# Fourteen column tiles of an input projection, in pairs by seven block products

## The reference

```
p   = x @ w_in                      # 1024 x 1024 times 1024 x 3072
y_A = RWKV-7 time mixing of p[:, :1408]      (token shift, delta rule)
y_B = Griffin RG-LRU of p[:, 1408:1920]      (conv of width 4, gates, scan)
y_C = stick-breaking attention of the rest   (q, k, v of 384 columns each)
x   = LayerNorm(alpha * x + concat(y_A, y_B, y_C) @ w_out)
x   = LayerNorm(alpha * x + grouped top-2 MoE(x))
```

## Time and profile before

| | us |
|---|---|
| median of three runs | 1342.16 |
| the profiled execution | 1342.95 |
| its span, first to last instruction | 1341.2 |
| PE busy | 1242.6 |
| DVE busy | 468.9 |
| ACT busy | 381.1 |
| POOL busy | 121.0 |
| matmuls of the column tiles (L205) | 293.9 |

### The profile page before, as it was taken

The page is one execution under the profiler, slowest core; times in us unless marked ns, Lnnn a source line. Parts: engine busy times, 40 slices in busy tenths (PEclk is TensorE's granted clock), DMA queues, the critical chain, the costliest instruction groups (busy, mean ns, idle before and its releaser), DMA issues.

```text
span 1341.2 us, 23288 instructions
## 1 busy us (share of the span) xinstructions
PE 1242.6 (93%) x9734; PEld 602.4 (45%) x9734; DVE 468.9 (35%) x833; ACT 381.1 (28%) x571; POOL 121.0 (9%) x206
## 2 busy tenths in 40 slices
PE   7999999999989999998999956999999999999980
PEld 3444444444557777775445532333333333333320
DVE  3035301244357777774364353111111111111117
ACT  1034402333145565555222122111111111111114
POOL 1000000000021221220000001010101010101010
PEclk9999999999989999999999977999999999999995
DMA  5110001010000001001704019776799499397226
GB/s 220 32 47 31 32 32 47 32 31 16 0 2 3 34 4 34 4 3 65 267 6 157 28 44 354 275 273 197 268 313 312 148 319 367 101 369 254 55 38 259
DMA packets 61013, 170.19 MB, mean 127 GB/s; under 512 B 3184, under 2 KB 3312, under 8 KB 60928
## 3 DMA queue, kind: packets, MB, share of 16 engines
q1 hardware_dynamic: 54384, 145.31, 29.0%
q0 software_dynamic: 6544, 23.63, 7.4%
HBM read 144.29 MB, written 24.64 MB: 126 GB/s over the span
## 4 chain that ended last, share of the span: by engine, by line
PE 84%; DVE 6%; DMA 4%; ACT 3%; issue 2%; POOL 0%; SPq 0%; POOLq 0%; DVEq 0%; ACTq 0%
PE PS L1829 31%; PE PS L205 19%; PE PS L1300 8%; PE PS L214 3%; PE PS L659 3%; PE PS L994 2%; PE PS L678 2%; PE PS L1003 2%; PE PS L1013 2%; PE PS L1822 2%; DMA YT<-x1d,RK 1%; PE PS L348 1%; PE PS L1440 1%; PE PS L734 1%; DMA XS<-in_xT 1%
## 5 line engine op out<-in xcount | busy, mean ns | idle before, releaser
L205 PE MATMUL PS<-XS 128*128 128x512 f32 x672 | 293.9, 597 | 7.6 <-DMA XS<-in_xT 7.1
L1829 PE MATMUL PS<-XS,YT 128*64 128x512 f32 x656 | 287.9, 596 | 3.5 <-DMA SQ<-in_w_upx 2.6
L1829 PE MATMUL PS<-SQ,YT 128*64 128x512 f32 x488 | 216.4, 597 | 0.0
L1829 PE MATMUL PS<-RK,YT 128*64 128x512 f32 x672 | 211.1, 593 | 0.0
L205 PEld LDWEIGHTS PS<-XS 128*128 128x128 f32 x672 | 127.1, 191 | 172.7 <-issue 163.9
L1829 PEld LDWEIGHTS PS<-XS,YT 128*64 128x64 f32 x656 | 88.9, 137 | 185.4 <-issue 180.8
L1300 PE MATMUL PS<-SQ,YT 128*128 128x512 f32 x256 | 114.0, 594 | 0.6 <-issue 0.6
L1917 DVE TENSOR_TENSOR YT<-YT,PS 128x256 f32<-128x256 f32 x42 | 15.8, 418 | 274.7 <-PE PS L1829 274.7
L1829 PEld LDWEIGHTS PS<-RK,YT 128*64 128x64 f32 x672 | 65.9, 137 | 74.7 <-issue 74.7
L1300 PEld LDWEIGHTS PS<-SQ,YT 128*128 128x128 f32 x256 | 47.7, 190 | 56.7 <-issue 56.5
L1829 PEld LDWEIGHTS PS<-SQ,YT 128*64 128x64 f32 x488 | 66.4, 138 | 0.0
(11 more groups left out here) (386 smaller groups left out, 1591.2 us busy)
## 6 DMA issues: line engine op xcount, KB each, us to landing
RK<-in_w_down SPq DMA_DIRECT2D x6, 2048.0 KB, 12.6
XS<-in_w_in SPq DMA_DIRECT2D x21, 512.0 KB, 3.3
XS<-in_w_gate SPq DMA_DIRECT2D x5, 2048.0 KB
XS<-in_w_upx SPq DMA_DIRECT2D x5, 2048.0 KB
XS<-in_w_down SPq DMA_DIRECT2D x5, 2048.0 KB
RK<-in_w_gate SPq DMA_DIRECT2D x5, 2048.0 KB, 19.7
SQ<-in_w_gate SPq DMA_DIRECT2D x4, 2048.0 KB
RK<-in_w_upx SPq DMA_DIRECT2D x4, 2048.0 KB, 19.7
```

Of the source, the lines that this page charges most:

```text
L205: m = e.matmul(acc[:, half * HB:(half + 1) * HB], XS[:, 8 + n % 4, kt * P:(kt + 1) * P], XS[:, kt, half * HB:(half + 1) * HB], start=kt == ...
L1829: ins = e.matmul(acc[r, :], rows[:, r], third_cols(n, k, at, HB), start=start, stop=stop)
```

## The change

Two column tiles a (= n) and b (= n + 1) are computed together for n = 0, 2, ..., 12, that is for the tiles 0 to 13. The 256 columns by 1024 tokens are seen as a 2 by 2 block product: the contraction is cut into channels 0 to 511 and 512 to 1023 (a1, a2 of tile a; b1, b2 of tile b), the tokens into two halves. Instead of eight block products it takes seven (the Winograd form of Strassen's scheme), each of four matmuls 128x128 by 128x512 into one PSUM quarter of 512 columns. The four quarters of PS0 and PS1 are used in turn, one for each product.

- `x_sums` on DVE, ahead of `masks_dve`: sixteen subtractions of 128x512 give four sums of quarters of x, kept in SQ[:, 0:8].
- `weight_sums` on POOL, seven times: four additions or subtractions of 128x512 for each pair.
- `pair_pe` makes the seven products; `pair_act` copies the first from PSUM; `pair_dve` adds the six others to the rows in SBUF with seven TENSOR_TENSOR of 128x512 (product 4 is added twice).
- The RWKV rows lie in YT or TT now, not in PSUM, when ACT and DVE make the token shift.
- The load of w_in tile 1 is issued between x tiles 3 and 4.
- The pieces of LRU and RWKV after tile n run inside the pair: on PE after the second product (n) and after the fourth (n + 1); on ACT both after the copy of the first product; on DVE ahead of the additions (n) and after the fifth of them (n + 1).
- Seven semaphores are renamed or reused; tiles 14 to 20 and the v columns are computed as before.

```diff
-                if ct == 0:
-                    for kt in range(KT):
+                if ct < 2:
+                    for kt in range(4 * ct, 4 * ct + 4):
                         e.dma_start(XS[:, kt, :], t["xT"][kt]).then_inc(s_x[kt], 16)
...
+        def x_sums(e):
+            for k in range(4):
+                wait(e, s_x[k], 16)
+                e.tensor_tensor(XSUM[0][:, k, :], XQ[0, 1][:, k, :], XQ[0, 0][:, k, :], ALU.subtract).then_inc(s_ts, 1)
+            for k in range(4):
+                wait(e, s_x[4 + k], 16)
+                wait(e, s_ts, 4 + k)
+                e.tensor_tensor(XSUM[1][:, k, :], XQ[1, 1][:, k, :], XSUM[0][:, k, :], ALU.subtract).then_inc(s_ts, 1)
+            for k in range(4):
+                e.tensor_tensor(XSUM[2][:, k, :], XQ[1, 1][:, k, :], XQ[0, 1][:, k, :], ALU.subtract).then_inc(s_ts, 1)
+            wait(e, s_ts, 8)
+            for k in range(4):
+                e.tensor_tensor(XSUM[3][:, k, :], XQ[1, 0][:, k, :], XSUM[1][:, k, :], ALU.subtract).then_inc(s_ts, 1)
+
+        def weight_sums(e, p):
+            n, a1, a2, b1, b2, s1, s2, s4 = weights_of(p)
+            for i in range(2):
+                wait(e, s_w[(n + i) % 4], 16 * ((n + i) // 4 + 1))
+            if p >= 2:
+                wait(e, s_pp, n - 2)
+            e.tensor_tensor(s1, b1, b2, ALU.add).then_inc(s_ss, 1)
+            wait(e, s_ss, 4 * p + 1)
+            e.tensor_tensor(s2, s1, a1, ALU.subtract).then_inc(s_ss, 1)
+            wait(e, s_ss, 4 * p + 2)
+            e.tensor_tensor(b1, a1, b1, ALU.subtract).then_inc(s_ss, 1)
+            e.tensor_tensor(s4, a2, s2, ALU.subtract).then_inc(s_ss, 1)
+
+        def pair_pe(e, p, after):
...
+            product(0, a1, XQ[0, 0]).then_inc(s_mp, 1)
...
+            product(1, a2, XQ[1, 0]).then_inc(s_mp, 1)
+            after(n)
+            wait(e, s_w[(n + 1) % 4], 16 * ((n + 1) // 4 + 1))
+            wait(e, s_ts, 8)
+            wait(e, s_ss, 4 * (p + 1))
+            wait(e, s_md, 7 * (p - 1) + 6)
+            product(2, s2, XSUM[1]).then_inc(s_mp, 1)
+            wait(e, s_ts, 12)
+            wait(e, s_md, 7 * p)
+            product(3, b1, XSUM[2]).then_inc(s_mp, 1)
+            after(n + 1)
+            wait(e, s_me, p + 1)
+            product(4, s1, XSUM[0]).then_inc(s_mp, 1)
+            wait(e, s_ts, 16)
+            wait(e, s_md, 7 * p + 2)
+            product(5, b2, XSUM[3]).then_inc(s_pp, 1)
+            wait(e, s_md, 7 * p + 1)
+            product(6, s4, XQ[1, 1]).then_inc(s_pp, 1)
+
+        def pair_act(e, p, after):
...
+            wait(e, s_mp, 5 * p + 1)
+            wait(e, s_pd, r)
+            e.copy(A[:, 0:HB], quarter(p, 0)).then_inc(s_me, 1)
+            after(n)
+            after(n + 1)
+            if r >= 0:
+                wait(e, s_derived, 1)
+                wait(e, s_md, 7 * (p + 1))
+                for i, x in enumerate((A, B)):
+                    e.activation(RW[:, r + i, :], x, ACT.Identity, scale=v1(V_NMU + r + i)).then_inc(s_pa, 1)
+
+        def pair_dve(e, p, after):
...
+            after(n)
+            wait(e, s_me, p + 1)
+            wait(e, s_mp, 5 * p + 3)
+            add(A[:, HB:S], 2, A[:, 0:HB])
+            wait(e, s_md, d0 + 1)
+            add(A[:, 0:HB], 1, A[:, 0:HB])
+            wait(e, s_mp, 5 * p + 4)
+            wait(e, s_pd, r)
+            add(B[:, 0:HB], 3, A[:, HB:S])
+            wait(e, s_mp, 5 * p + 5)
+            wait(e, s_md, d0 + 3)
+            add(B[:, HB:S], 4, B[:, 0:HB])
+            add(A[:, HB:S], 4, A[:, HB:S])
+            after(n + 1)
+            wait(e, s_pp, n + 1)
+            wait(e, s_md, d0 + 5)
+            add(B[:, 0:HB], 5, B[:, 0:HB])
+            wait(e, s_pp, n + 2)
+            add(A[:, HB:S], 6, A[:, HB:S])
+            if r >= 0:
+                for i, x in enumerate((A, B)):
+                    wait(e, s_pa, r + i + 1)
+                    e.scalar_tensor_tensor(RW[:, r + i, 1:S], x[:, 0:S - 1], v1(V_MU + r + i), RW[:, r + i, 1:S],
+                                           ALU.mult, ALU.add).then_inc(s_pd, 1)
...
         def _(e):
             masks_pool(e)
+            for p in range(PAIRS):
+                weight_sums(e, p)
             mats_pool(e)
...
         def _(e):
+            x_sums(e)
             masks_dve(e)
             lru = [lru_dve(e, u) for u in range(2)]
```

More of the change, by code:

```diff
@@ L115, in layer_kernel @@
         s_masksd = sem("masks_built_dve")
-        s_x = [sem(f"x_loaded{i}") for i in range(NT)]
+        s_x = [sem(f"x_or_sums_loaded{i}") for i in range(NT)]
         s_w = [sem(f"w_in_loaded{i}") for i in range(4)]
@@ L121, in layer_kernel @@
         s_pe = sem("proj_copied_by_act")
+        s_ts, s_ss = sem("x_sums_dve"), sem("weight_sums_pool")
+        s_mp, s_me, s_md = sem("quarter_products_in_psum"), sem("quarters_copied_act"), sem("quarters_added_dve")
         s_ld, s_la, s_lp = sem("lru_dve"), sem("lru_act"), sem("lru_pe")
@@ L149, in layer_kernel @@
         s_ya, s_yd, s_ys = sem("y_act"), sem("y_dve"), sem("y_stored")
-        s_gt = [sem(f"sums_loaded{i}") for i in range(NT)]
         s_tick = [sem("sp_passed_wait"), sem("pool_passed_wait")]
@@ L185, in proj_sp @@
                 e.dma_start(XS[:, 8 + k, :], t["w_v"][:, (k - 1) * S:k * S]).then_inc(s_w[k], 16)
-        def proj_free(e, n):
[L189 to L194, removed]
+        FIRST_PAIR, PAIRS = 0, 7
+        XSUM = [SQ[:, 2 * i:2 * i + 2, :].rearrange("p a b -> p (a b)").rearrange("p (k c) -> p k c", k=4) for i in range(4)]
@@ new lines, in layer_kernel, with weights_of, pair_rows @@
+        XQ = {(j, k): XS[:, 4 * j:4 * j + 4, k * HB:(k + 1) * HB] for j in range(2) for k in range(2)}
+        WSUM = YT[:, 0:3, :].rearrange("p a b -> p (a b)").rearrange("p (s i c) -> p s i c", s=2, i=3)
+        def weights_of(p):
+            n = FIRST_PAIR + 2 * p
+            a, b = [XS[:, 8 + (n + i) % 4, :] for i in range(2)]
+            s1, s2, s4 = [WSUM[:, p % 2, i, :] for i in range(3)]
+            return n, a[:, 0:HB], a[:, HB:S], b[:, 0:HB], b[:, HB:S], s1, s2, s4
+        def pair_rows(p):
+            n = FIRST_PAIR + 2 * p
+            return (YT[:, 3 + n, :], YT[:, 4 + n, :]) if n < LRU_T else (YT[:, 7, :], TT[:, 2, :])
@@ new lines, in quarter, with product @@
+        def quarter(p, i):
+            q = 7 * p + i + 1
+            return PS[q // 2 % 2][:, q % 2 * HB:(q % 2 + 1) * HB]
+        def pair_pe(e, p, after):
+            n, a1, a2, b1, b2, s1, s2, s4 = weights_of(p)
+            def product(i, left, right):
+                for k in range(4):
+                    m = e.matmul(quarter(p, i), left[:, k * P:(k + 1) * P], right[:, k, :], start=k == 0, stop=k == 3)
+                return m
+            wait(e, s_md, 7 * (p - 1) + 3)
+            wait(e, s_w[n % 4], 16 * (n // 4 + 1))
+            if p == 0:
+                for k in range(4):
+                    wait(e, s_x[k], 16)
+            product(0, a1, XQ[0, 0]).then_inc(s_mp, 1)
+            wait(e, s_md, 7 * (p - 1) + 5)
+            if p == 0:
+                for k in range(4, KT):
+                    wait(e, s_x[k], 16)
+            product(1, a2, XQ[1, 0]).then_inc(s_mp, 1)
[16 more added lines that the diff above has]
+            product(6, s4, XQ[1, 1]).then_inc(s_pp, 1)
@@ new lines, in pair_act @@
+        def pair_act(e, p, after):
+            n, r = FIRST_PAIR + 2 * p, FIRST_PAIR + 2 * p - LRU_T
+            A, B = pair_rows(p)
+            wait(e, s_mp, 5 * p + 1)
[8 more added lines that the diff above has]
+                    e.activation(RW[:, r + i, :], x, ACT.Identity, scale=v1(V_NMU + r + i)).then_inc(s_pa, 1)
@@ new lines, in pair_dve, with add @@
+        def pair_dve(e, p, after):
+            n, r = FIRST_PAIR + 2 * p, FIRST_PAIR + 2 * p - LRU_T
+            A, B = pair_rows(p)
+            d0 = 7 * p
+            def add(to, i, other):
+                e.tensor_tensor(to, quarter(p, i), other, ALU.add).then_inc(s_md, 1)
+            after(n)
[22 more added lines that the diff above has]
+                                           ALU.mult, ALU.add).then_inc(s_pd, 1)
@@ new lines, in pair_at, with paired @@
+        def pair_at(n):
+            p = (n - FIRST_PAIR) // 2
+            return p if (n - FIRST_PAIR) % 2 == 0 and 0 <= p < PAIRS else None
+        def paired(n):
+            return FIRST_PAIR <= n < FIRST_PAIR + 2 * PAIRS
+        def proj_free(e, n):
+            m = n - 2
+            if paired(m):
+                wait(e, s_md, 7 * PAIRS - 1)
+            elif LRU_T <= m < RW_END:
+                wait(e, s_pd, m - LRU_T + 1)
+            elif m >= RW_END:
+                wait(e, s_pe, m - RW_END + 1)
@@ L201, in proj_pe @@
                 for half in range(2):
+                    if half and paired(n - 2):
+                        wait(e, s_md, 7 * PAIRS)
                     for kt in range(KT):
@@ L261, in own @@
                 wait(e, s_ld, n[0])
-            wait(e, s_pe, LRU_T)
+            wait(e, s_md, 14)
             own()
@@ L989, in sba_pe @@
```

(39 more changed lines are left out.)

## The result

The changed kernel takes 1353.25 us (median of four runs, 1353.16 to 1355.20), the kernel before 1342.66 us (four runs, 1341.47 to 1344.11). The ratio is 1.0084, with a 95% interval of 1.0069 to 1.0099: slower by 10.6 us. The profiled execution took 1353.28 us, its span is 1351.5 us. The forecast was 1347.5 us in 1337 to 1354. The direction and the kind of mechanism held. The size did not: the kernel lost 10.6 us where 4.8 were forecast, outside the forecast's own 1345 to 1350, and the time is that of rival 2, in which VectorE and GpSimd wait for each other in full (1353).

The account below looks back on a forecast made before the run. PE's matmuls were taken to bound the kernel. Pairs 0 and 1 +11.7 - 3.4, pairs 2 to 4 +4.0, pairs 5 and 6 -6.9 gave +5.4 us, median 1347.5 us, range 1337 to 1354.

Parts of the forecast that it names:

- rival 2: DVE and POOL wait for each other in full: +11 us after pair 1, 1353 us in all; chance 0.14.
- The saved work: Projection on PE: a pair takes 24.0 us where two tiles took 27.5; seven pairs save 24.0 us.
- The start: Pair 0: PE stands 7.4 us before P5, behind DVE's sums of x and masks; +8.3 us after pair 1.
- POOL beside DVE: Pairs 0 and 1: POOL's weight sums delay DVE's sums of x by 2.5 us, bounds 0 and 5 us.
- with all: End of pair 0 at 53 us as upper bound, where 50.3 us was forecast.
- The clock: PE after each long wait: 1.7 us for half clock, bounds nothing and twice that.
- Rival 3: Clock stays at 2.4 GHz over the three waits and POOL finds gaps: -4.1 us, 1338 us; chance 0.11.
- Pairs 2 to 4: Pairs beside the LRU: save 10.3 us of matmuls, lose 14.3 us to waits of 3.7 and 8.4 us and clock.
- The sum: All terms up to tile 14: +11.7 - 3.4 + 4.0 - 6.9 = +5.4 us.
- Given back: After tile 14: the prediction had what follows unchanged and shifting with PE, so nothing given back.
- Rival 1: POOL does not delay DVE: +1.0 us in all, 1343.2 us, counted as no change; chance 0.22.
- Rival 4: DVE's queue does not hold PE, only saved matmuls count: 24.0 less 3.4 us, 1321.6 us; chance 0.05.

Follow-up runs that it names:

- e9: e8 with the mask building in two parts, between the additions of P4 and P5 of pair 0 and after its last addition: 1321.19 us.
- e6: Changed kernel with masks_dve between the additions of pair 0 and those of pair 1: 1344.5 us, ratio 1.0011 to the kernel before.
- e5: Changed kernel without GpSimd's weight sums, so the projection is wrong: 1366.6 us, not comparable; tile 14 starts at 218.05 us, not 227.87.
- e4: Changed kernel with fourteen more float32 matmuls into an unused PSUM quarter between P4 and P5 of pair 0: 1352.55 us.
- e1: Changed kernel with masks_dve ahead of x_sums on VectorE: 1349.08 us, ratio 1.0059 to the kernel before.
- e7: Changed kernel with masks after pair 0's additions, GpSimd's pair 1 sums held, and the LRU's second half one tile later: 1329.48 us.
- e8: e7 with the convolution of the LRU's second half one place later on VectorE, behind the additions of P4 of pair 3: 1324.53 us.
- e2: Changed kernel with GpSimd's weight sums of pair 1 held until the second addition of pair 0: 1350.39 us, ratio 1.0063 to the kernel before.
- e3: Changed kernel with the LRU's second half tied to tiles 8, 9, 10 and not 7, 8, 9: 1339.43 us, ratio 0.9979 to the kernel before.

## Why the prediction was right, and where its sizes were off

**The saved work** is as forecast: pair 1, without a wait, goes from 54.79 to 78.82 us, 24.0 us. e9 shows that all seven pairs can run without a hole behind the arrival of x.

**The start.** P1, which needs the last tile of x, starts at 18.28 us (18.1 forecast). The order of DVE's queue is the cause of the hole (e6), and without POOL the hole is 7.1 us (e5; 7.4 forecast). The term that was mis-sized is the lock, "POOL beside DVE": 2.5 us were taken, 5.5 measured. The row of a scan that lost 0.46 us was read as the price of a meeting. By the times in the rows it was more likely one caught halfway, since the scan began at 396.02 us and the POOL copies behind it only at 396.62; this was not tested. In the changed kernel eight subtractions lost about 4.3 us to POOL's four sums of pair 1, about one microsecond for each sum. Pair 0 ended at 54.79 us, 4.5 us after the 50.3 forecast: 3.0 us are the lock, 1.3 us the clock. It also ended after the 53 us that the prediction gave as its worst case, "with all". That sum holds the lock in full but the clock at 1.7 us only, although the clock's own bound was twice that.

The Trainium skill (SBUF — State Buffer, section Summary: rules for kernel authors) says of a DVE instruction with two SBUF inputs and a GpSimd instruction that reads SBUF that the second one to issue "fully blocks" until the first finishes. Measured, DVE lost 1.0 us to a POOL sum of 1.27, so this wording gave the better price. Rival 2, built on it, met the time in part by luck: it had 11 us after pair 1 and 7 over pairs 2 to 4, and 12.7 and 6.0 were measured.

**The clock.** Forecast 1.7 us for each long wait, 5.1 in all; by the distances in PE's timeline it was 3.0, 1.4 and 2.5 us, 6.9 in all. e4 takes 2.9 us off at the first hole. Rival 3, that the clock stays, is out for these three waits. The 1.7 us came from the spacing of the first records at the kernel's start, where the profile's granted clock reads 1.00, so that row had not shown a price of the half clock.

**Pairs 2 to 4.** Pair 3 took 35.2 us (106.63 to 141.81), forecast 35.1; pair 4 took 37.8, forecast 36.1. The holes of 4.2 and 9.2 us were forecast as 3.7 and 8.4. From the end of pair 1 to that of pair 4 it is 100.8 us, forecast 98.8, before 94.8. Of these 2.0 us, 1.2 are the longer holes and 0.5 the clock. Behind the holes stands the lock again: the second token shift took 2.29 us instead of 1.28 in both pairs, and e5, without POOL, has holes of 3.2 and 7.3 us.

**The sum** at tile 14: 5.4 forecast, 4.5 more at the start and 2.0 more in pairs 2 to 4 give 11.9 us, where 12.1 were measured. The 0.2 us are about what starts in the timeline and in the chain differ by.

**Given back.** The prediction let what follows tile 14 shift with PE. With 12.1 us and nothing given back the time would have been about 1354.7 us, outside the range of 1337 to 1354; that the measured time is inside it is owed to this stretch, which nobody forecast. From tile 14 to the delta rule the two kernels run alike. In its first block they do not. The first and second block's POOL work, before and after the change:

```profile
373.00 1.62 POOL L617 TENSOR_TENSOR XS<-RK,pc 128x384 f32<-128x384 f32 x2 [367.69 <-PE PS L214]
395.05 1.62 POOL L617 TENSOR_TENSOR XS<-RK,pc 128x384 f32<-128x384 f32 x2 [17.66 <-PE PS L734]
```
```profile
385.05 1.62 POOL L762 TENSOR_TENSOR XS<-RK,pc 128x384 f32<-128x384 f32 x2 [195.73 <-PE PS L359]
405.87 1.63 POOL L762 TENSOR_TENSOR XS<-RK,pc 128x384 f32<-128x384 f32 x2 [16.42 <-PE PS L879]
```

The block takes 22.05 us before and 20.82 after. PE stands in it for about 3.2 us in both. Before, the clock read 0.50 when it went on the earlier trace rows; in the changed kernel it read 1.00 for the first two microseconds (same columns as above):

```profile
390.00:392.00 2.00, 1.69 (x44) 1.00 0.00 0
392.00:394.00 2.00, 1.40 (x41) 0.53 0.04 8
```

It fell some two microseconds of work later. That this is why the block is shorter is read from the rows and not tested. Nothing in the change aims at it; e1 to e7 have 22.4 to 22.6 us for the block, e9 22.05 and e8 21.0. It is part of why times and tile 14 differ by 1 to 2 us between kernels; another half microsecond came back after this block and was not followed. What decides when the clock falls here was not tried.

**Rival 1** (POOL does not delay DVE) is out by e2 and e5. **Rival 4** was wrong for this kernel; e9 reaches its size once the queues are in order.

## What to carry to other kernels

A product saved on the bound engine is worth its time only while each piece queued on the helpers still comes in time; list, for each engine in order, what stands ahead of the instruction that PE waits for, and move that. Work that was free because it lay under a transfer (here the masks) is no longer free once something is put ahead of it. Give each meeting of a POOL instruction with DVE instructions that read only SBUF nearly the whole POOL instruction as its price: here it was 1.0 us of 1.27. For a hole in PE, reckon with half clock behind it as a possible extra. The holes of 2.0 to 12.7 us in these runs cost 1.4 to 3.0 us more than their length, but the one of 3.2 us in e6 cost nothing more, so the length of a hole alone does not tell.

## What the runs showed of the hardware that I had not expected

- A DVE instruction of 0.23 us with a single tensor operand (a CAST, a TENSOR_SCALAR) stood 1.25 us beside a POOL sum, as the two-operand ones did. An addition with one operand in PSUM did not: at 28.89 us in e8 it took 0.69 us in the middle of four POOL sums, which took 1.26 or 1.27 us each; e7 and e9 show the same.
- After a hole of 12.7 us dense float32 matmuls ran at a granted clock of 0.50 (1.2 GHz) for about 6 us.
- After a hole of 2.0 us a product took 5.2 us instead of 3.43 (P5 of pair 3 in e7, 116.96 to 122.16 us; the same in e3), and after the longer hole of 3.2 us in pair 1 of e6 it took 3.51 us with the clock at 1.00.
